# First layer: projections, attention and output projection rebuilt, with attention units taken by key group and long and short tiles in turn

## The chip, the cores and the metric

One core of one Trainium2 chip runs the whole program in one launch. The metric is the device time of that core in microseconds; the value for a kernel is the median of its runs.

## The reference, cut to what matters

The network has a first block of two layers and then a second block with routed experts. The change lies in layer 0 of the first block, up to the entry of its feed-forward part. There are 256 tokens (`x`) and 256 context rows (`ctx`), each 1024 wide, so four tiles of 128 rows.

```python
hx = rms_norm(x, norm1_g[layer]) * (1.0 + sc1) + sh1        # the same for ctx with its own sc, sh
q, k, v = split(h @ w_in)                                   # 1024 -> 16*64 | 4*64 | 4*64
q, k = rms_norm(q, q_gain), rms_norm(k, k_gain)             # per head of 64
qx, kx = apply_axial_rope(...)                              # tokens only
# tokens: 4 heads of each key group against 256 token keys (|i-j| <= 128) and 256 context keys, with a sink
# context: against the 256 context keys, with a sink
x = x + g1 * (o @ w_out);  ctx = ctx + cg1 * (oc @ w_out)
hx2 = rms_norm(x, norm2_g[layer]) * (1.0 + sc2) + sh2       # entry of conv_glu
```

`sh`, `sc` and `g` come from `silu(c) @ ada_w + ada_b`: per layer 12 column blocks of 512, so 24 weight blocks of 2 MB for both layers.

## The kernel before, in words

Weights stream through a ring of three 2 MB slots in SBUF. One queue, SyncE's, issues all loads in a written order; a load waits until the slot's previous weights have been used, and everything behind it in the queue waits too. PSUM has eight banks. `plan` code gives every group of results a number; a group uses bank number modulo 8, and TensorE's `bank(key)` waits until the reader of the group eight before has read it. `do` in the vector and scalar programs waits for each instruction's own end before the next.

Stages of layer 0, in TensorE's order:

1. Four `ada` blocks (`ada`, `ada2`): the modulation of layer 0's first norm. VectorE then squares, sums and scales the four tiles (`rms`), TensorE turns them (`turn`), ScalarE scales and shifts the turned halves (`norm_turn`, 32 instructions).
2. Projection: block 0 of `w_in` as fp32 matmuls (`stay`), blocks 1 and 2 as four half blocks of 256 columns, each product taken as three products of a high and a low part (`qw_high`, `hw_low`, `qx_high`, `qx_low`).
3. Per tile, VectorE norms the 20 heads of q and k, multiplies by the gains and applies the rotation in 12 small instructions (L1903 to L1928); TensorE turns them (L1017).
4. Attention: 16 units in the order of tiles, four key groups each. The eight of the token tiles are long (512 keys), the eight of the context tiles short (256 keys). `attention` is software pipelined: in step i TensorE does the scores of unit i, then the turning of unit i-1's exponentials and the product with v. After each unit one further `ada` block is done (`ADA_BETWEEN`). The sum of exponentials divides the result at the end (L1802).
5. The result is turned (`o0`), and the output projection (`project`) runs as fp32 matmuls of 128x512; then gate, residual sum (`residual`), norm, turn, modulation and split into high and low parts, one after another, and the feed-forward part begins at L841 with `hT_high`, `w_split`.

## Time and profile before

| | us |
|---|---|
| median of 3 runs | 2844.99 (2839.59 to 2847.72) |
| the profiled execution's own time | 2848.02 |
| its span | 2846.2 |
| TensorE busy | 2477.9 (87%) |
| VectorE busy | 974.3 (34%) |
| ScalarE busy | 775.1 (27%) |
| first matmul of the feed-forward part of layer 0 | at 495.12 |

The span is the time from the first to the last instruction of the profiled execution. "Idle before" stands in brackets behind a row of the timeline with what ended it. A busy TensorE is not TensorE at its full clock: the column PEclk tells the granted clock, 1.00 for 2.4 GHz throughout and 0.50 for 1.2 GHz.

### The profile page before, as it was taken

The page shows a single profiled execution, that of the slowest core. Times are in us where ns is not written, and L with a number is a line of the kernel's source. Part 1 is how long each engine was busy: PE and PEld are TensorE (multiplying, and loading weights), DVE is VectorE, ACT ScalarE, POOL GpSimd, SP SyncE. Part 2 cuts the span into 40 slices and gives each one's busy share as a digit, 9 for nine tenths or more (in the row PEclk, how much of TensorE's full clock was granted, in tenths as well). Part 3 has the DMA queues.
Part 4 walks back from the last instruction along what each step waited for, and adds up shares of the span by engine and source line. Part 5 has one row for each costly group of instructions (what it writes and reads, how often), then busy time and mean ns, then how long its engine had stood idle before and what let it go on. Part 6 is the DMA issues. An engine that isn't in the chain of part 4 may idle for free.

```text
span 2846.2 us, 31745 instructions
## 1 busy us (share of the span) xinstructions
PE 2477.9 (87%) x12956; PEld 1613.8 (57%) x12956; DVE 974.3 (34%) x1419; ACT 775.1 (27%) x1248; POOL 4.2 (0%) x6
## 2 busy tenths in 40 slices
PE   4939886999997997757999989799999999999995
PEld 2726653778785897654988986343333333334332
DVE  1274423334414238773654343341111111111112
ACT  2223533223314245433543453111111111111110
POOL 0000000000000000000000000000000000000000
PEclk8968997999997999887999997989999999999998
DMA  8103540442222140021555430569999999999993
GB/s 305 60 30 119 206 149 30 163 147 90 89 74 89 60 148 1 1 89 60 178 181 201 168 104 1 204 267 428 428 429 429 428 421 422 429 429 417 421 429 161
DMA packets 141897, 603.55 MB, mean 212 GB/s; under 512 B 6272, under 2 KB 51584, under 8 KB 117088
## 3 DMA queue, kind: packets, MB, share of 16 engines
q1 hardware_dynamic: 141792, 602.10, 53.5%
q8 instruction: 73, 1.20, 0.2%
q14 instruction: 32, 0.26, 0.0%
HBM read 601.03 MB, written 1.05 MB: 212 GB/s over the span
## 4 chain that ended last, share of the span: by engine, by line
PE 73%; DMA 10%; DVE 8%; ACT 6%; issue 2%; SPq 1%; ACTq 0%; DVEq 0%
PE bank L841 70%; DMA arena<-in_b_up 10%; ACT hT L1362 1%; PE bank L912 1%; DVE arena L2022 1%; ACT modp L1362 1%; ACT arena L1399 1%; DMA ring<-in_ada_w 1%; ACT arena L1387 1%; DVE xn L1742 1%; PE bank L873 0%; ACT modp L1338 0%; ACT hT L1376 0%; DVE modp L2012 0%; DVE xn L2011 0%
## 5 line engine op out<-in xcount | busy, mean ns | idle before, releaser
L841 PE MATMUL bank<-arena 128*64 128x512 f32 (+5 forms) x3088 | 644.2, 488 | 77.6 <-ACT arena L1692 25.7
L841 PEld LDWEIGHTS bank<-arena 128*64 128x64 f32 (+2 forms) x3088 | 340.5, 175 | 337.2 <-issue 267.5
L841 PE MATMUL bank<-ring,arena 128*64 128x512 f32 (+1 forms) x1632 | 394.9, 608 | 23.8 <-DMA arena<-in_b_up 21.0
L841 PE MATMUL bank<-hT_high,w_split 128*128 128x512 f32 (+1 forms) x1408 | 351.1, 341 | 30.4 <-issue 30.4
L841 PEld LDWEIGHTS bank<-ring,arena 128*64 128x64 f32 (+1 forms) x1632 | 141.3, 143 | 269.6 <-issue 259.7
L841 PEld LDWEIGHTS bank<-hT_high,w_split 128*128 128x128 f32 x1408 | 245.2, 192 | 60.6 <-issue 32.6
L841 PE MATMUL bank<-hT_low,w_split 128*128 128x512 f32 (+1 forms) x704 | 238.5, 339 | 0.0
L2159 DVE TENSOR_SCALAR arena<-bank 128x512 f32<-128x512 f32 x32 | 22.1, 692 | 549.5 <-PE bank L841 549.5
L841 PE MATMUL bank<-ring,hT 128*128 128x512 f32 (+1 forms) x432 | 182.6, 584 | 17.7 <-ACTq L666 17.7
L841 PEld LDWEIGHTS bank<-ring,hT 128*128 128x128 f32 x432 | 81.4, 195 | 116.6 <-issue 97.2
L841 PEld LDWEIGHTS bank<-hT_low,w_split 128*128 128x128 f32 x704 | 135.4, 192 | 15.3 <-issue 1.5
L755 DVE TENSOR_TENSOR w_split<-ring,w_split 128x1024 fp32r<-128x1024 f32 x88 | 107.8, 1225 | 23.2 <-ACT w_split L1417 21.3
L1417 ACT ACTIVATE w_split<-ring 128x1024 fp32r<-128x1024 f32 x88 | 93.4, 1062 | 57.9 <-PE bank L841 56.0
L2163 DVE TENSOR_SCALAR arena<-bank 128x512 f32<-128x512 f32 x32 | 22.1, 692 | 222.9 <-PE bank L841 222.9
L1688 ACT ACTIVATE arena<-arena 128x512 f32<-128x512 f32 x32 | 20.1, 629 | 246.4 <-DVE arena L2159 246.4
L841 PE MATMUL bank<-down_high,hid_high 128*128 128x512 f32 x216 | 84.9, 393 | 0.0
L841 PE MATMUL bank<-down_low,hid_high 128*128 128x512 f32 x216 | 84.0, 389 | 0.0
L841 PE MATMUL bank<-down_high,hid_low 128*128 128x512 f32 x216 | 84.0, 389 | 0.0
L1695 ACT ACTIVATE arena<-bank 128x512 f32<-128x512 f32 x32 | 19.1, 597 | 232.6 <-PE bank L841 232.6
L1679 ACT ACTIVATE arena<-bank 128x512 f32<-128x512 f32 x34 | 18.4, 594 | 208.3 <-PE bank L841 208.3
L1973 DVE TENSOR_TENSOR hw_low<-ring,hw_high 128x2048 fp32r<-128x2048 f32 x18 | 41.3, 2292 | 97.1 <-ACT hw_high L1514 96.9
L841 PEld LDWEIGHTS bank<-arena,xn 128*128 128x128 f32 x544 | 64.1, 197 | 15.5 <-issue 15.5
(307 smaller groups left out, 3418.6 us busy)
## 6 DMA issues: line engine op xcount, KB each, us to landing
ring<-in_w_gate SPq DMA_DIRECT2D x64, 2048.0 KB
arena<-in_w_down SPq DMA_DIRECT2D x64, 2048.0 KB, 15.1
ring<-in_w_up SPq DMA_DIRECT2D x32, 2048.0 KB
arena<-in_w_up SPq DMA_DIRECT2D x32, 2048.0 KB
ring<-in_ada_w SPq DMA_DIRECT2D x24, 2048.0 KB, 7.9
ring<-in_ffn_w_up SPq DMA_DIRECT2D x44, 1024.0 KB, 7.7
ring<-in_w_in SPq DMA_DIRECT2D x11, 2048.0 KB, 8.0
ring<-in_ffn_w_down SPq DMA_DIRECT2D x10, 2048.0 KB, 7.7
```

The costliest lines, as they stand in the source:

```text
L755: then(eng.tensor_tensor(w[:, 1, :, g, :], raw, w[:, 0, :, g, :].bitcast(F32), ALU.subtract))
L841: return pe.matmul(o, l, r, start=start, stop=stop)
L912: m = pe.transpose(ps[:, j * P:(j + 1) * P], pr[:, r * n + j * P:r * n + (j + 1) * P], ident)
L1362: do(act.activation(o, ps[:, j * P:(j + 1) * P], ACT.Identity, bias=modT[:, l, 24 * i + k, v:v + 1], scale=coef[:, l, i, k, v:v + 1]), F i ...
L1387: do(act.activation(PT[:, r % 2, 0:u["n"]], ps[:, 0:u["n"]], ACT.Copy), F)
L1399: do(act.activation(pr, pr, ACT.Exp, bias=st[:, 4 + r:5 + r], accum_out=st[:, 12 + r:13 + r]))
L1417: do(act.activation(w_split[fc % 2][:, 0, :, g, :], raw[:, :, g, fc % 2, :], ACT.Copy), w_high)
L1742: do(dve.tensor_tensor_reduce(out=xn[:, t % 2, :], in0=xr[:, t, :], in1=xr[:, t, :], scale=1.0, scalar=0.0, op0=ALU.mult, op1=ALU.add, acc ...
L1973: do(TT(hw_low[:, slot_of[unit_no[key]], :, 256 * z:256 * z + 256], raw, hw_high[j % 2][:, :, :].bitcast(F32), ALU.subtract), hw_low_ready)
L2022: do(dve.copy_predicated(rA[:, t, :, :], m, ps), F)
L2159: dve.tensor_scalar(hm[:, :], PS[0][:, :], 7.0, None, ALU.min).then_inc(hm_ready, 1)
L2163: link(dve.tensor_scalar(um[:, :], PS[1][:, :], 7.0, -7.0, ALU.min, ALU.max))
```

## The change

- The order of loads: x and ctx go first, the first constants are cut to 998 columns, score masks and level masks follow in front of the third block of `w_in`. The norm of x and ctx is taken before the modulation arrives, into a region of its own for each tile (`xn4`).
- Modulation of the turned tiles is shared: ScalarE takes the first halves, VectorE the second; each tile is split into high and low parts as soon as it is done.
- All three blocks of `w_in` are taken as six half blocks with the three products, keys and values first (`Q_BLOCKS`). Norm and rotation of keys run beside the projection of queries; tables of gain times cosine and sine are made once (`rope`). Queries' scale 1/rms goes into the exponential's scale (`stat` columns 0 to 63).
- Attention: units by key group, in each the tiles 0, 2, 1, 3 (token, context, token, context). Keys and queries lie in 64 rows each, so a score matmul has 64 rows (upper or lower half in turn). VectorE adds the mask and takes the maximum in one instruction. Scores of a context unit stay in their two banks until ScalarE has taken the exponentials from there (reader `exp`). The exponentials are divided by their sum before they are turned; turning goes by key chunk with four heads together, and v is the stationary operand, 64 columns at a time, so the result comes out turned and is split at once (`o_high`, `o_low`).
- The two blocks of `w_out` are loaded during attention (after units 10 and 13) and hold slots 0 and 2; the last `ada` blocks then have slot 1 alone. The output projection uses the three products. Gate, norm, turn and modulation go tile by tile behind the last output block (`enter_first`).
- For `ada` blocks that hold gates (4, 5, 10, 11) the small turning group `adat` is dropped.

```diff
+        ATT0, ATT2 = [(t, g) for g in range(NKV) for t in (0, 2, 1, 3)], list(att_units2())
 
         ADA_BETWEEN = [(0, 4 + i // 2) if i % 2 == 0 else (1, (0, 1, 2, 3, 6, 7, 8, 9)[i // 2]) for i in range(16)]
         ADA_LATE = [4, 5, 10, 11]
-        plan_att(ATT0, lambda i: plan_ada(*ADA_BETWEEN[i]))
-        plan_turn("o0", ALL)
-        for b in range(2):
-            col_unit(("wo0", b), a["attn_w_out"][0], b * 512)
-            for t in ALL:
-                add(("wo0", b, t), "dve")
+        WO_AFTER = {10: 0, 13: 1}
+
+        def out_unit(b):
+            w = a["attn_w_out"][0].rearrange("(m s j d) n -> s d m j n", m=NKV, s=2, j=2)
+            stream(("wo0", b), *[(lambda s, z=z, m=m: ring_col(s, 0, 512)[64 * z:64 * z + 64, 2 * m:2 * m + 2, :],
+                                  w[z, :, m, :, b * 512:(b + 1) * 512]) for z in range(2) for m in range(NKV)])
+
+        for i in range(len(ATT0) + 1):
+            if i < len(ATT0):
+                t, g = ATT0[i]
+                for r in range(4 if t < XT else 2):
+                    add(("score", t, g, r), "dve" if t < XT else "exp")
+            if i:
+                t, g = ATT0[i - 1]
+                l, blk = ADA_BETWEEN[i - 1]
+                ada_turn[l, blk] = len(ada_turn) % 2
+                col_unit(("ada", l, blk), a["ada_w"][l], blk * 512)
+                add(("adap", l, blk), "act")
+                for c in range(NT if t < XT else NT - XT):
+                    add(("probt", t, g, c), "act")
+                add(("pv", t, g), "dve")
+                plan_ada2(l, blk)
+                if i - 1 in WO_AFTER:
+                    out_unit(WO_AFTER[i - 1])
...
-            s = [x for x in order if x < RING - 1 or not narrow][0] if key != ("hq", 0) else RING - 1
+            held = [] if key[0] != "ada" else [slot_of[unit_no["wo0", b]] for b in range(2)
+                                               if ("wo0", b) in names[:n] and names[n - 1][0] != "up"]
+            s = [x for x in order if (x < RING - 1 or not narrow) and x not in held][0]
+            s = {("hq", 0): RING - 1, ("wo0", 0): 0, ("wo0", 1): RING - 1}.get(key, s)
...
+            early = {1: (constants,), 6: (score_masks, level_masks), 7: (gate_biases,)}
             sp.dma_start(cols[:, :], a["cols"]).then_inc(cols_landed, 16)
+            tokens()
             for n, pieces in enumerate(units):
...
+            def q_half(j):
+
+                key, z = Q_HALVES[j]
+                s = unit(key)
+                hi, lo = qw_high[j % 3], hw_low[:, s, :, 256 * z:256 * z + 256]
                 parts = [(k, *p) for k in range(KC) for p in ((hi, qx_high), (hi, qx_low), (lo, qx_high))]
+                pe.wait_ge(qw_low_ready, j + 1)
                 for t in ALL:
-                    ps = bank((*key, t))
+                    if j == 0:
+                        pe.wait_ge(qx_low_ready, t + 1)
+                    g = ("kv", t) if key[1] == 2 else ("q", key[1], t)
+                    ps = bank(g)
                     for n, (k, wt, x) in enumerate(parts):
                         m = mm(ps[:, 256 * z:256 * z + 256], x[:, k, t * P:(t + 1) * P], wt[:, k, :], n == 0,
                                n == len(parts) - 1)
                     if z:
-                        close(m, (*key, t))
-                if z:
-                    release(m)
+                        close(m, g)
+                    elif t == NT - 1:
+                        m.then_inc(q_half_used, 1)
...
+            def scores(t, g):
+                tok = slice(t * P, (t + 1) * P)
+                lo = 0 if t < XT else SEQ
+                ps = [bank(("score", t, g, r)) for r in range(4 if t < XT else 2)]
+                for r in range(4):
+                    half = slice(64 * (r % 2), 64 * (r % 2) + 64)
+                    o = ps[r][:, :] if t < XT else ps[r % 2][:, 256 * (r // 2):256 * (r // 2) + 256]
+                    m = mm(o, qT[half, 2 * g + r // 2, tok], kT[half, g, lo:TOK], True, True)
+                    if t < XT:
+                        close(m, ("score", t, g, r))
+                    elif r > 1:
+                        close(m, ("score", t, g, r - 2))
+
+            def weighted(i):
+                t, g = ATT0[i]
+                chunks = NT if t < XT else NT - XT
+                pr = P0[:, i % 2, :, :]
+                await_next(p_ready)
+                for c in range(chunks + 1):
+                    if c < chunks:
+                        ps = bank(("probt", t, g, c))
+                        for r in range(4):
+                            m = pe.transpose(ps[:, r * P:(r + 1) * P], pr[:, r, c * P:(c + 1) * P], ident)
+                        close(m, ("probt", t, g, c))
+                    if c:
+                        await_next(pt_ready)
+                        if c == 1:
+                            pv = bank(("pv", t, g))
+                        at = c - 1 if t < XT else c - 1 + XT
+                        for s in range(2):
+                            m = mm(pv[64 * s:64 * s + 64, 0:256], v0[:, at, g * HD:(g + 1) * HD],
+                                   PT0[:, (c - 1) % 2, 256 * s:256 * s + 256], c == 1, c == chunks)
+                close(m, ("pv", t, g))
+
+            for i in range(len(ATT0) + 1):
+                if i < len(ATT0):
+                    scores(*ATT0[i])
+                if i:
+                    ada(*ADA_BETWEEN[i - 1])
+                    weighted(i - 1)
+                    ada2(*ADA_BETWEEN[i - 1])
+
+            pe.wait_ge(o_low_ready, len(ATT0))
+            for b in range(2):
+                s = unit(("wo0", b))
+                for t in ALL:
+                    ps = bank(("wo0", b, t))
+                    for z in range(2):
+                        j = 2 * b + z
+                        pe.wait_ge(wo_low_ready, j + 1)
+                        hi, lo = wo_high[j], hw_low[:, s, :, 256 * z:256 * z + 256]
+                        parts = [(k, *p) for k in range(KC) for p in ((hi, o_high), (hi, o_low), (lo, o_high))]
+                        for n, (k, wt, x) in enumerate(parts):
+                            m = mm(ps[:, 256 * z:256 * z + 256], x[:, k, t * P:(t + 1) * P], wt[:, k, :], n == 0,
+                                   n == len(parts) - 1)
+                    close(m, ("wo0", b, t))
+                    if b and t:
+                        turn(("f", 0), (t - 1,), lambda t: xn[:, t % 2, :], lambda t: await_next(xn_ready))
+            turn(("f", 0), (NT - 1,), lambda t: xn[:, t % 2, :], lambda t: await_next(xn_ready))
...
+            def enter_first():
+
+                for t in range(NT + 1):
+                    if t < NT:
+                        std(t, 1)
+                    if t == 0:
+                        await_next(coef_ready)
+                    if t == 2:
+                        weights_high(0, 0)
+                    if t:
+                        norm_turn(("f", 0), (t - 1,), 0, 1, split=True, stds=False)
...
+            for i in range(len(ATT0) + 1):
+                if i:
+                    t, g = ATT0[i - 1]
+                    ada(*ADA_BETWEEN[i - 1])
+                    for c in range(NT if t < XT else NT - XT):
+                        ps = take(("probt", t, g, c))
+                        do(act.activation(PT0[:, c % 2, :], ps[:, :], ACT.Copy), F)
+                        signal(pt_ready)
+                    pe_past(("pv", t, g))
+                    do(act.activation(o_high[:, 2 * g:2 * g + 2, t * P:(t + 1) * P],
+                                      PS[group["pv", t, g] % BANKS][:, 0:256].rearrange("p (j q) -> p j q", j=2),
+                                      ACT.Copy), o_high_ready)
+                    if i - 1 in (13, 14):
+                        out_high(i - 14)
+                if i == len(ATT0):
+                    continue
+                t, g = ATT0[i]
+                st = stat[:, 64 + 32 * (i % 2):96 + 32 * (i % 2)]
+                if i == 0:
...
-                            o = kT[64 * z:64 * z + 64, z::2, t * P:(t + 1) * P]
-                            do(act.activation(o, ps[64 * z:64 * z + 64, :, :], ACT.Copy), F if z else act_step)
-            signal(qT_ready)
-
-            def with_ada(i):
-                ada(*ADA_BETWEEN[i])
-
-            attention(ATT0, with_ada)
-            plain_turn("o0", ALL)
+                        pr = P0[:, i % 2, r, 0:CTX]
+                        src = PS[group["score", t, g, r % 2] % BANKS][:, 256 * (r // 2):256 * (r // 2) + 256]
+                    at = t * NH + 4 * g + r
+                    do(act.activation(pr, src, ACT.Exp, bias=st[:, 4 + r:5 + r], scale=stat[:, at:at + 1],
+                                      accum_out=st[:, 12 + r:13 + r]))
+                if t >= XT:
...
+            def enter_first():
+
+                coefs(0, 1)
+                for t in ALL:
+                    gated_add(("wo0", 0, t), 0, t, GATE[(0, 0)], tmp=region(1024, 512))
+                for t in range(NT + 1):
+                    if t < NT:
+                        gated_add(("wo0", 1, t), 1, t, GATE[(0, 0)], tmp=region(1024, 512))
+                        rms(("f", 0), (t,))
+                    if t == NT - 1:
+                        signal(gates_read)
+                    if t == 2:
+                        weights_low(0, 0)
+                    if t:
+                        split_tokens(t - 1)
+
...
+            for i in range(len(ATT0) + 1):
+                if i:
+                    t, g = ATT0[i - 1]
+                    st = stat[:, 64 + 32 * ((i - 1) % 2):96 + 32 * ((i - 1) % 2)]
+                    n = TOK if t < XT else CTX
+                    await_next(sum_ready)
+                    do(TT(st[:, 12:16], st[:, 12:16], st[:, 8:12], ALU.add))
+                    do(dve.reciprocal(st[:, 16:20], st[:, 12:16]))
+                    for r in range(4):
+                        pr = P0[:, (i - 1) % 2, r, 0:n]
+                        do(dve.tensor_scalar(pr, pr, st[:, 16 + r:17 + r], None, ALU.mult),
+                           p_ready if r == 3 else dve_step)
+                if i < len(ATT0):
+                    t, g = ATT0[i]
+                    st = stat[:, 64 + 32 * (i % 2):96 + 32 * (i % 2)]
+                    if t < XT:
+                        for r in range(4):
+                            ps = take(("score", t, g, r))
+                            do(dve.tensor_tensor_reduce(out=P0[:, i % 2, r, :], in0=ps[:, :],
+                                                        in1=C("mask0", t * 512, 512), scale=1.0, scalar=-3e38,
+                                                        op0=ALU.add, op1=ALU.max, accum_out=st[:, r:r + 1]), F)
+                    else:
+                        for z in range(2):
+                            pe_past(("score", t, g, z))
+                            ps = PS[group["score", t, g, z] % BANKS][:, :].rearrange("p (h c) -> p h c", h=2)
+                            do(dve.tensor_reduce(st[:, z:4:2], ps, AX, ALU.max))
+                    at = t * NH + 4 * g
+                    do(TT(st[:, 0:4], st[:, 0:4], stat[:, at:at + 4], ALU.mult))
+                    do(STT(out=st[:, 4:8], in0=st[:, 0:4], scalar=-1.0, in1=minus_sink[:, 4 * g:4 * g + 4],
+                           op0=ALU.mult, op1=ALU.min))
+                    do(TT(st[:, 8:12], ROW("sink", 4 * g, 4), st[:, 4:8], ALU.add), max_ready)
+                if i:
+                    t, g = ATT0[i - 1]
+                    cut = (slice(None), slice(2 * g, 2 * g + 2), slice(t * P, (t + 1) * P))
+                    ps = take(("pv", t, g))[:, 0:256].rearrange("p (j q) -> p j q", j=2)
+                    await_next(o_high_ready)
+                    do(TT(o_low[cut], ps, o_high[cut].bitcast(F32), ALU.subtract), F)
+                    signal(o_low_ready)
+                    ada2(*ADA_BETWEEN[i - 1])
+                    if i - 1 in (14, 15):
+                        out_low(i - 15)
```

## Rows read from the trace of the kernel before

**Rows 1.** Windows: us, busy time (instructions) by engine, PEclk, DMA share, GB/s.
```profile
9.20:44.00 34.80, 20.70 (x96) 8.77 (x96) 0.69 (x4) 2.39 (x4) 0.00 (x0) 1.00 1.00 383
44.00:72.00 28.00, 7.92 (x33) 6.27 (x32) 10.04 (x19) 16.66 (x37) 0.00 (x0) 0.52 0.54 202
101.00:148.00 47.00, 46.95 (x387) 46.27 (x385) 2.98 (x2) 4.79 (x9) 0.00 (x0) 1.00 0.26 90
148.00:200.00 52.00, 11.29 (x48) 9.69 (x48) 40.30 (x56) 11.33 (x21) 0.00 (x0) 0.57 0.11 41
200.00:320.00 120.00, 107.89 (x632) 72.95 (x632) 57.41 (x106) 52.27 (x112) 0.00 (x0) 0.91 0.36 123
320.00:396.00 76.00, 66.74 (x467) 44.81 (x466) 34.50 (x93) 38.51 (x113) 0.00 (x0) 1.00 0.63 222
403.00:461.00 58.00, 56.90 (x128) 24.81 (x128) 10.51 (x16) 1.32 (x2) 0.00 (x0) 0.97 0.00 1
461.00:495.00 34.00, 7.58 (x32) 5.98 (x32) 16.08 (x27) 23.14 (x47) 0.00 (x0) 0.56 0.17 62
```
**Rows 2.** Chain that ended last, in order of time: start us, us, what.
```profile
12.22 20.52 DMA ring<-in_ada_w
72.52 75.44 PE bank L841 x448
310.71 0.82 ACT arena L1399 x2
403.13 56.91 PE bank L841 x128
476.23 0.64 ACT hT_high L1366
478.86 0.64 ACT hT_high L1366
495.12 23.87 PE bank L841 x96
```
**Rows 3.** Timeline of TensorE: start us, us, engine line op out<-in xcount.
```profile
57.85 1.97 PE L873 MATMUL bank<-const,xn 128*128 128x128 f32 x8 [0.74 <-DVE xn L1747]
241.05 1.92 PE L841 MATMUL bank<-ring,cT 128*32 128x512 f32 x16
243.74 1.05 PE L841 MATMUL bank<-const,modp 128*128 128x2 f32 x8 [0.76 <-ACTq L666]
244.65 3.68 PE L841 MATMUL bank<-arena 128*128 128x512 f32 x8
248.17 1.04 PE L912 MATMUL bank<-const,arena 128*128 128x128 f32 x8
254.10 1.92 PE L841 MATMUL bank<-ring,cT 128*32 128x512 f32 x16
```
**Rows 4.** Timeline of TensorE among the experts: operands of 64 rows, then 64 columns.
```profile
2002.29 1.99 PE L841 MATMUL bank<-arena 64*128 64x512 f32 x8
2013.01 7.07 PE L841 MATMUL bank<-ring,arena 128*64 128x512 f32 x32
```
**Rows 5.** Groups by form up to 820 us: count, busy us, mean ns, idle before.
```profile
L1783 DVE TENSOR_TENSOR arena<-bank,const 128x512 f32<-128x512 f32 x32 | 22.1, 691 | 13.8 <-PE bank L841 13.7
L1742 DVE CUSTOM_DVE_ANT_0 xn<-xr 128x1024 f32<-128x1024 f32 x8 | 9.8, 1226 | 0.3
L1747 DVE TENSOR_SCALAR xn<-xr,stat 128x1024 f32<-128x1024 f32 x8 | 6.0, 753 | 0.3
L1888 DVE TENSOR_TENSOR hw_low<-ring,qw_high 128x2048 fp32r<-128x2048 f32 x3 | 6.9, 2292 | 0.1
L1399 ACT ACTIVATE arena<-arena,stat 128x256 f32<-128x256 f32 x32 | 16.2, 508 | 1.7
L1387 ACT ACTIVATE arena<-bank 128x512 f32<-128x512 f32 x32 | 19.1, 597 | 32.9 <-PE bank L912 32.0
```
**Rows 6.** One window of layer 1's recurrence, columns as in rows 1.
```profile
1150.00:1200.00 50.00, 34.62 (x255) 32.49 (x256) 37.95 (x45) 23.95 (x50) 0.00 (x0) 0.90 0.00 1
```

563 lines of the change are left out of this document (371 added, 192 removed).

## The prediction

> **What bounds the kernel now.** I read the windows first, by stage. Only the stretch before 495.12, the first matmul of the feed-forward part, is rebuilt; what follows keeps its instructions and, but for slots 0 and 1 changing roles, its loads. In that stretch TensorE is full in three stages alone: projection (46.95 us of 47), attention (107.89 of 120, then 66.74 of 76) and output projection (56.90 of 58). Between them it is nearly empty: 7.92 of 28 us at 44 to 72, 11.29 of 52 at 148 to 200, 7.58 of 34 at 461 to 495, and there its granted clock is 0.52 to 0.57, mostly the lower level of 1.2 GHz [rows 1]. Before 44 the DMA engines are full at 383 GB/s [rows 1]; the third ada block lands at 12.22 + 20.52 = 32.74 [rows 2]. The chain passes through TensorE from 72.52 for 75.44 us and from 403.13 for 56.91 us [rows 2]. So the bounds are loads, then TensorE, and in the gaps VectorE's and ScalarE's chains.
>
> **The change part by part.** All sums are made in the profiled execution's time (span 2846.2, its own time 2848.0); the median shown lies 3.0 below that.
>
> **A, until the first projection matmul, 72.5 before.** Everything that landed before the third ada block was 11.2 MB (cols, four of constants, x, ctx and masks, three ada blocks). Now 2.0 MB of masks come later, so the fourth block is behind 11.3 MB and lands at about 33 (0.1 MB more at 0.383). Its matmuls (twice 1.92 [rows 3], at the low clock), a copy of 0.6, the small turning of 1.05 [rows 3] and coefficients 0.2 take 5.7 with issue: 38.7, less what a warm start would save, 38.2. x and ctx are already normed. TensorE turns four tiles in 4 x 1.97 [rows 3] and is through at 46.1. A half tile has a rhythm of 2.62: one split copy of 0.64 and four instructions of 0.49 [rows 2]. ScalarE now has 4 x 0.49 + 2 x 0.65 = 3.3 per tile, the other half being VectorE's, so from 40.5 the tiles are ready every 3.3 us while a tile's product takes 2.9; TensorE can start at 46.1 and never waits long. A = -26.4.
>
> **B, projection, 75.4 before** [rows 2]. Six half blocks, 4 tiles, 24 matmuls each, at 46.95 / 387 = 0.12 us [rows 1]: 69.1. Turning keys and first queries, 32 x 0.12 = 3.9. The fifth half block waits for banks of the turned keys: ScalarE has a query tile (1.3), a 1.9 us split and a copy ahead, about 2.0 net. Start at the low clock after the 0.52 stretch [rows 1]: 2.0, which is 4 us at half rate; bounds none and 6. B = 77.0, +1.6. The splits on VectorE (2.29 each [rows 5]) lie beside 11.5 us of TensorE each.
>
> **C, from the last projection to the first score, 52.1 before.** Norm and rotation of keys and of the first half of queries now lie beside B. What is left: copy and square of the last context tile 1.3, its sum 0.7, root 0.4, four copies of 0.64 (0.597 [rows 5] and issue) 2.5. C = 4.9, -47.2. If the rotation of the second queries were not hidden, 3 us more.
>
> **D, attention, 203.1 before (200.05 to 403.13).** Matmuls of 64 rows, two halves in turn, take 1.99 us per 8 of 512 columns [rows 4] against 3.68 for 128 rows [rows 3]: scores of a long unit 2.0. Products with 64 stationary columns take 7.07 / 32 = 0.22 per 512 columns [rows 4], so 0.11 for 256. ada 1.85, 16 transposes 2.0 (1.04 per 8) [rows 3]. TensorE's sum is about 9 for a long and 6 for a short unit, 15 per pair; before, a long unit took 254.10 - 241.05 = 13.05 [rows 3] and a short one about 9 (76 us for some eight and a half [rows 1]). But a chain is longer than that, because division now comes ahead of turning. Let E(i) be the end of unit i's exponentials.
>
> Step from a long unit to a short one: sum, reciprocal and four scalings of 512 at 0.42 (half of 753 ns and issue [rows 5]) 2.15; turning of the first chunk 0.7; four copies 2.6; last product 0.75; o_high 0.47; four exponentials of 256 (0.508 [rows 5] and accumulator) 2.53 and a small one 0.25: 9.45. Scaling is bounded by 0.2 (nothing in the trace so short for 512) and 0.69 [rows 5]; I take the half of L1747 since both read SBUF.
>
> Step from a short unit to a long one: the scores of a short unit stay in two banks until E. In the order of groups the `adat` or first `adag` group of the long unit before is eight behind the short unit's first score, and the next long unit's first score eight behind the second score. So TensorE stands until E and then does, in order, ada2 (1.05 [rows 3], 1.8 where it is two gate products of 512), scores 2.04, ada 1.85, turning 0.7, two copies 1.3, product 0.75, o_high 0.45, then ScalarE four exponentials of 512 at 0.845 (0.82 and issue [rows 2]) 3.4 and 0.25: 11.95, with gates 12.7. VectorE's maximum-with-mask (1226 ns for 1024 [rows 5], I take 0.8; bounds 0.6 and 0.9) is behind TensorE there and costs nothing but in the first unit.
>
> First unit 8.5; eight steps of 9.45 = 75.6; four of 11.95 and three of 12.7 = 85.9; two splits of w_out ahead of exponentials 3.9; the end, with ada2(14), ada(15) and a low-part split (2.29 [rows 5]) ahead of the last scaling, 11.0. Sum 184.9. TensorE idles some 3 us per pair in one piece, and is busy 15 of 21.7; a stage busy 34.62 of 50 is granted 0.90 [rows 6], the long units 0.91 with their cold start [rows 1]. About 8 us of a pair's chain is TensorE's; at 0.96 that is 6 us over all, at 0.90 it is 14, at 1.00 none. D = 190.9, -12.2. The loads: one 2 MB block per unit of 10 us needs 2.1 / 0.383 = 5.5 us [rows 1], so the ring keeps pace; with slot 1 alone, blocks 14 and 15 are loaded 8 us after their predecessor's use, about when wanted.
>
> **E, output projection, 56.9 before** [rows 2]: 384 matmuls at 0.12 = 46.1, -10.9 with the gap ahead. The three splits' times lie beside it.
>
> **F, to the feed-forward part, 35.0 before.** ScalarE's rhythm of 2.62 per half tile stays [rows 2]. From the end of output tile 1 (11.5 before E's end) VectorE and ScalarE go in turn: VectorE's `split_tokens(t-1)` waits for `norm_turn(t-1)`, and the next tile's gate and square wait behind it. Tile 1: gate and add 2 x 0.7 and square 1.3 ([rows 5], L1783's and L1742's kinds) 2.75, root 0.35, two half tiles 5.25, low part 0.7: 9.1; tile 2 the same and 2.2 for weights_high: 11.3; tile 3: 9.1; the last modulation 5.4. Sum 34.9, less 11.5: 23.4. F = -11.6.
>
> Sum: -26.4 + 1.6 - 47.2 - 12.2 - 10.9 - 11.6 = -106.7. 2848.0 - 106.7 = 2741.3, and against the median 2738.
>
> **The rivals.**
> (1) The banks held by the exponentials cost nothing (TensorE is ahead by other work, the step short to long falls to 10 us): 7 x about 2.2 = -15, and scaling at 0.2 gives -7 more: 2716 to 2723. For it: TensorE idled only 0.76 us ahead of the small turning in a steady unit before [rows 3]. Against: the group numbers are fixed by the plan.
> (2) The clock falls in attention. TensorE's 15 us per pair are in pieces with 2 to 3.4 us between them; the stage 148 to 200, busy 11.29 of 52, was granted 0.57 [rows 1]. With half of the pairs' time at 1.2 GHz: 8 pairs x 8 us x 0.5 = +32, less the 6 in the sum: 2764; all of it: 2796. The Trainium skill ("TensorE: Matmul & The Clock Gate", its decision table) says that throughput drops mid-kernel are avoided only without idle gaps between bursts of matmuls; by that rule the clock would fall in every pair, which is this rival. So far the trace speaks against it at this duty (0.90 at 69% busy [rows 6]).
> (3) The two row halves don't run side by side in scores: 8 long units at 3.68 in place of 2.0 [rows 3, 4], +14: 2752. [rows 4] speak against it: there the same kind of matmul in alternating halves took 0.25 each.
> (4) The held slots leave the ring without lead, and each unit waits for its ada block: a landing costs some 8 us after issue; exposed at all 16 units it is 16 x 8 = +128 and the kernel is slower, 2866. It decides from 106.7 / 16 = 6.7 us per unit. Against it: slots are held only from unit 11 on, where at most 5 units can be hit (+40: 2778).
>
> **How the numbers follow.** The forecast 0.60, (1) 0.14, (2) 0.14, (3) 0.07, (4) 0.02 in full, other mishaps 0.03. Bounds of unknown costs around the forecast: scaling -7 to +9, clock -6 to +8, A and B 5 each way. Range 2708 to 2772. A measurement here tells 0.3% or 8 us from no change; the gain exceeds it in all cases but (4) and a mishap of three figures: faster 0.96, same 0.01, slower 0.03.
>
> **What would show it.** First projection matmul at 46, first score at 128, output projection from 319 to 365, first matmul of the feed-forward part at 388. In attention, TensorE should idle before ada2 or scores with ScalarE's exponential as releaser, once per pair; pairs should take about 21.8 us, and PEclk stay above 0.9. ScalarE's and VectorE's turns after output tile 1 should be about 9 us per tile. I am wrong if the pair takes under 20 or over 25 us, if the clock there is below 0.8, or if the part after 495 before does not come out equal.

## The result and the profile after

The changed kernel takes 2778.55 us (median of 4 runs, 2776.03 to 2780.76) against 2845.52 before: ratio 0.9768 [0.975, 0.9785]. It is 67 us faster; 107 were forecast, and the range ended at 2772. The profiled execution has a span of 2778.9 and a time of its own of 2780.76, against a forecast of 2741.3 in those terms, so the miss is 39.4 us. The medians in the table of experiments take in every execution; two of them fell into a slower state, one of e12_best (4170.02 us) and one of the kernel before measured with e11_four_chunks and e12_best (4362.48), while the ratios leave such executions out.

| | before | forecast | after |
|---|---|---|---|
| first projection matmul | 72.52 | 46.1 | 45.62 |
| first score | 200.05 | 128.0 | 129.28 |
| first output-projection matmul | 403.13 | 318.9 | 363.45 |
| first matmul of the feed-forward part | 495.12 | 388.4 | 435.00 |
| from there to the end of the span | 2351.1 | 2351.1 | 2343.9 |

The row of attention is where it went wrong: 234.2 us where 190.9 were forecast and 203.1 were taken before.

The windows of after answer [rows 1], with the same columns (us, busy time by engine PE, PEld, DVE, ACT, POOL, granted clock, DMA share, GB/s). The first five are the stages, the last three a pair of units within attention.

```profile
9.20:44.00 34.80, 21.16 (x128) 10.37 (x128) 14.40 (x41) 10.03 (x17) 0.00 (x0) 0.95 1.03 381
45.60:124.00 78.40, 75.32 (x610) 74.55 (x611) 42.24 (x67) 32.57 (x51) 0.00 (x0) 0.98 0.33 119
129.60:363.40 233.80, 168.81 (x880) 78.83 (x879) 89.92 (x260) 103.83 (x228) 0.00 (x0) 0.79 0.43 138
361.00:408.00 47.00, 47.00 (x370) 46.27 (x367) 20.94 (x27) 10.57 (x16) 0.00 (x0) 0.93 0.26 90
408.00:435.00 27.00, 8.32 (x61) 7.48 (x60) 14.36 (x21) 18.71 (x36) 0.00 (x0) 0.70 0.11 39
...
244.80:251.90 7.10, 4.02 (x34) 2.07 (x32) 2.87 (x8) 4.81 (x11) 0.00 (x0) 0.96 0.84 297
251.90:268.30 16.40, 12.85 (x48) 6.98 (x48) 5.56 (x18) 5.60 (x14) 0.00 (x0) 0.60 0.53 106
268.30:279.30 11.00, 8.22 (x66) 3.74 (x64) 3.97 (x16) 6.61 (x14) 0.00 (x0) 1.00 0.62 204
```

Projection and output projection are full and hardly disturbed. Attention has a granted clock of 0.79, and it does not fall evenly: within the pair it is 0.60, so mostly 1.2 GHz, for 16.4 us and 1.00 right after. TensorE's timeline of that stretch shows what it did before (start, us, what; in brackets the idle time ahead and what ended it):

```profile
246.89 1.92 PE L899 MATMUL bank<-ring,cT 128*32 128x512 f32 x16
251.96 1.97 PE L1116 MATMUL bank<-const,arena 128*128 128x128 f32 x8 [3.14 <-DVE arena L2273]
253.86 1.12 PE L899 MATMUL bank<-arena 128*64 128x256 f32 x4
254.91 1.12 PE L1116 MATMUL bank<-const,arena 128*128 128x128 f32 x4
255.96 1.12 PE L899 MATMUL bank<-arena 128*64 128x256 f32 x4
257.01 1.12 PE L1116 MATMUL bank<-const,arena 128*128 128x128 f32 x4
258.06 1.45 PE L899 MATMUL bank<-arena 128*64 128x256 f32 x8
262.88 1.84 PE L899 MATMUL bank<-const,modp 128*128 128x2 f32 x8 [3.37 <-ACTq L717]
264.65 3.78 PE L899 MATMUL bank<-arena 64*128 64x512 f32 x8
268.36 1.92 PE L899 MATMUL bank<-ring,cT 128*32 128x512 f32 x16
```

There are two gaps in a pair. The first, 3.14, ends with the division (L2273) of a long unit's exponentials; the four divisions are 2.05 us of it. Five of the eight long units have it at 3.14 or 3.15 (the others 6.30, 1.51 and 0.16). The second, 3.37 in seven pairs, ends with ScalarE's last exponential of the short unit: these are the held banks. In this pair what comes behind each gap runs at half speed. The scores at 264.65 take 3.78 us where eight such matmuls took 1.99 in [rows 4]; the same 16 `ada` matmuls at 268.36 take 1.92 as in [rows 3], the clock being back. The long chunk row of turning and product (251.96 to 259.5) shows a second thing: TensorE takes a chunk's turning and the previous chunk's product in turn, 2.1 us a chunk, and ScalarE's copy waits for it:

```profile
253.11 0.60 ACT L1698 ACTIVATE arena<-bank 128x512 f32<-128x512 f32 x1 [3.14 <-PE bank L1116]
...
256.06 0.60 ACT L1698 ACTIVATE arena<-bank 128x512 f32<-128x512 f32 x1 [1.50 <-PE bank L1116]
258.16 0.60 ACT L1698 ACTIVATE arena<-bank 128x512 f32<-128x512 f32 x1 [1.50 <-PE bank L1116]
```

I had it the other way round, with ScalarE's 0.65 as the rhythm.

### The profile page after: what moved, and what is told of

Same layout as the page of the kernel before. It is cut to its first block, busy times and chain, and to the rows that moved or that the text cites. A ratio compares the mean times of both kernels' runs of the same rounds, so it can differ in the third digit from the quotient of the medians.

```text
span 2778.9 us, 32087 instructions
## 1 busy us (share of the span) xinstructions
PE 2432.5 (88%) x13052; PEld 1589.9 (57%) x13052; DVE 973.9 (35%) x1509; ACT 785.7 (28%) x1242; POOL 4.2 (0%) x6
## 4 chain that ended last, share of the span: by engine, by line
PE 71%; DMA 11%; ACT 8%; DVE 8%; issue 2%; SPq 0%; ACTq 0%; DVEq 0%
PE bank L899 69%; DMA arena<-in_b_up 10%; ACT arena L1720 2%; DMA ring<-in_ada_w 1%; PE bank L1116 1%; DVE arena L2395 1%; ACT modp L1486 1%; DVE arena L2273 1%; ACT arena L1698 1%; PE bank L933 1%; ACT hT L1486 1%; ACT arena L1523 1%; DVE xr L2061 0%; DVE modp L2385 0%; DVE xn L2384 0%
## 5 line engine op out<-in xcount | busy, mean ns | idle before, releaser
L899 PE MATMUL bank<-arena 128*64 128x512 f32 (+6 forms) x2896 | 616.7, 523 | 81.5 <-ACT arena L1934 25.7
L899 PEld LDWEIGHTS bank<-arena 128*64 128x64 f32 (+2 forms) x2896 | 292.3, 173 | 348.4 <-issue 269.8
L899 PE MATMUL bank<-ring,arena 128*64 128x512 f32 (+1 forms) x1632 | 394.9, 608 | 23.4 <-DMA arena<-in_b_up 21.1
L899 PE MATMUL bank<-ring,hT 128*128 128x512 f32 (+1 forms) x240 | 96.3, 563 | 2.9 <-ACTq L717 2.9
L899 PEld LDWEIGHTS bank<-ring,hT 128*128 128x128 f32 x240 | 43.9, 194 | 54.1 <-issue 50.2
## 6 DMA issues: line engine op xcount, KB each, us to landing
arena<-in_w_down SPq DMA_DIRECT2D x64, 2048.0 KB, 14.9
```

Of the source, the lines that this page charges most:

```text
L899: return pe.matmul(o, l, r, start=start, stop=stop)
```

## The experiments

My theory after the result: the shortfall in attention is the granted clock, which falls because each pair has two gaps of over 3 us, and a long-to-short step that is longer than forecast even at full clock. Rivals: the held banks alone (at any clock), the order of units itself, VectorE's division, and the `adat` groups.

In the table: the median, its ratio to the kernel before as measured beside it, the stage from about the first score to the first output-projection matmul (us) and the clock granted in it, and the steps between the starts of two units' exponentials (L long, S short). Two steps of each changed kernel also hold a split of `w_out` on ScalarE, some 1.9 us, and are not in the ranges. Stage, clock and steps are those of the one profiled execution.

| | median | ratio [95%] | stage, clock | L to S | S to L |
|---|---|---|---|---|---|
| after | 2778.55 | 0.9768 [0.975, 0.9785] | 233.8, 0.79 | 12.2 to 14.6 | 13.7 to 14.5 |
| e1_by_tile | 2751.05 | 0.9666 [0.9644, 0.9687] | 204.2, 0.87 | L to L 12.4 to 13.9 | S to S 10.7 to 11.9 |
| e2_released | 2741.69 | 0.9636 [0.9614, 0.9658] | 189.3, 0.89 | 13.2 to 14.6 | 8.8 |
| e3_warm | 2755.46 | 0.9681 [0.9659, 0.9702] | 211.0, 0.93 | 12.2 to 13.7 | 11.1 to 12.0 |
| e4_before_alternating | 2853.36 | 1.0028 [1.0016, 1.0041] | 209.6, 0.94 (before: 203.1, 0.95) | | |
| e5_one_scaling | 2755.98 | 0.9683 [0.9661, 0.9705] | 211.5, 0.85 | 10.7 to 12.5 | 12.7 to 14.3 |
| e6_adat_back | 2790.98 | 0.981 [0.9783, 0.9837] | 238.7, 0.79 | 12.2 to 14.6 | 13.7 to 16.2 |
| e7_released_by_tile | 2741.02 | 0.962 [0.9588, 0.9651] | 190.1, 0.89 | L to L 12.4 to 14.6 | S to S 8.7 to 9.2 |
| e8_released_warm | 2734.58 | 0.9598 [0.9569, 0.9628] | 184.2, 0.95 | mostly 12.2 | 8.8 |
| e9_released_by_tile_warm | 2737.04 | 0.9614 [0.9598, 0.963] | 187.0, 0.90 | L to L 12.4 to 14.4 | S to S 8.7 to 10.3 |
| e10_two_by_two | 2759.28 | 0.9696 [0.9679, 0.9712] | 212.0, 0.86 | 12.2 to 13.4; L to L 12.4 to 13.3 | 10.2 to 12.0; S to S 13.2 to 13.3 |
| e11_four_chunks | 2761.69 | 0.9714 [0.9696, 0.9731] | 214.2, 0.86 | mostly 11.2 | 12.7 to 14.9 |
| e12_best | 2721.41 | 0.957 [0.9542, 0.9599] | 180.0, 0.94 | 11.2 to 12.3 | 8.8 |

### Useless work on TensorE (e3_warm)

```diff
-                    ada(*ADA_BETWEEN[i - 1])
+                    full = ATT0[i - 1][0] < XT
+                    ada(*ADA_BETWEEN[i - 1], again=full)
                     weighted(i - 1)
+                    if full:
...
+                        for _ in range(3):
+                            mm(PS[group["adap", l, blk] % BANKS][:, :], ident, const[:, 0:512], True, True)
```

`full` is true behind a long unit. With `again`, `ada` issues its matmuls twice, the first time for nothing; the three others go into a bank whose results have been read, in the wait ahead of `ada2`.

> The changed kernel with useless TensorE work in its two gaps per pair of units: the ada block of each long unit is multiplied twice, and three matmuls of 128x512 go into the ada block's read bank before ada2 of each long unit. It computes the same. Clock theory: TensorE stands too often, the clock is granted only about 0.8 in attention and its pieces run at half rate; with the gaps filled the granted clock there is 0.95 or more and a pair falls from 27 to about 24.5 us: 2755 to 2765, faster by adding work. Rival (the clock is not what costs; the gap before ada2 ends with ScalarE's exponentials anyway): 1 to 3 us more per long unit, 2785 to 2800.

TensorE has 176 matmul instructions more to do, by the count of the trace (1056 against 880), and the kernel is 23.1 us faster than the change. The window of the stage, and a pair in TensorE's timeline:

```profile
130.50:341.50 211.00, 176.95 (x1056) 79.10 (x1057) 89.93 (x260) 103.92 (x228) 0.00 (x0) 0.93 0.47 153
```

```profile
203.74 1.02 PE L899 MATMUL bank<-const,modp 128*128 128x2 f32 x8 [0.60 <-ACTq L717]
204.69 1.99 PE L899 MATMUL bank<-arena 64*128 64x512 f32 x8
206.61 1.92 PE L899 MATMUL bank<-ring,cT 128*32 128x512 f32 x16
208.46 1.09 PE L1118 MATMUL bank<-const,arena 128*128 128x128 f32 x8
...
218.48 1.09 PE L1118 MATMUL bank<-const,arena 128*128 128x128 f32 x8 [1.42 <-DVE arena L2281]
```

The gaps are 0.60 and 1.42 now, the small turning 1.02 (after: 1.84) and the scores 1.99 (3.78). VectorE's and ScalarE's busy times are those of after, so nothing but the clock and the filled gaps can have given the time. The step S to L is 11.1 us and 12.0 with gates: the forecast's step (11.95 from end to end of two units' exponentials is 11.08 from start to start, as a short unit's are 0.87 us shorter than a long one's). So that step was sized rightly for the full clock, held banks included, and the rest of it was the clock. L to S is 12.2 at the shortest where the forecast's 9.45 is 10.3: 1.9 too short at full clock. e3 does not reach that in each step: the mean of seven is 12.9, at a granted 0.93 in the stage (0.95 or more was expected). The row halves do run side by side (1.99).

### The held banks (e2_released) and the division (e5_one_scaling)

```diff
-                    add(("score", t, g, r), "dve" if t < XT else "exp")
+                    add(("score", t, g, r), "dve")
...
-                            pe_past(("score", t, g, z))
-                            ps = PS[group["score", t, g, z] % BANKS][:, :].rearrange("p (h c) -> p h c", h=2)
+                            ps = take(("score", t, g, z))[:, :].rearrange("p (h c) -> p h c", h=2)
                             do(dve.tensor_reduce(st[:, z:4:2], ps, AX, ALU.max))
+                            do(dve.tensor_copy(P0[:, i % 2, z:4:2, 0:CTX], ps), F)
```

> The changed kernel, but VectorE copies a short unit's scores from its two banks into SBUF (two copies of 512, about 1.4 us more per short unit on VectorE) and ScalarE takes the exponentials from there, so the banks are free early. Held-bank theory: TensorE does ada2 and the long scores during the short exponentials and no longer stands 3.4 us; 7 steps lose 3 to 5 us each, and the clock is granted more than the 0.8 it has in attention: 2745 to 2760. Rival (VectorE's and ScalarE's chain is what counts, TensorE is only late because it is allowed to be): within 4 us of the changed kernel, 2775 to 2782.

VectorE has 11 us more to do (100.96 busy against 89.92) and the kernel is 36.9 us faster. The step S to L falls from 13.7 or more to 8.8; L to S does not move. TensorE's gap ahead of the small turning and the scores is gone, the one ahead of a long unit's turning is left:

```profile
212.82 1.09 PE L1116 MATMUL bank<-const,arena 128*128 128x128 f32 x8 [3.49 <-DVE arena L2269]
...
219.46 1.05 PE L899 MATMUL bank<-const,modp 128*128 128x2 f32 x8
220.44 1.99 PE L899 MATMUL bank<-arena 64*128 64x512 f32 x8
```

The seven steps S to L of the profiled execution are 37 us shorter together, which is the whole gain. In e3 the same seven steps take 82.3 us, here 63.1: 19 are the wait at full clock (2.3 a step, 3.3 where the block holds gates), which the forecast had as a cost of the change (rival (1), that it would not be there, took 15 off for it). The other 18 go with the clock, which is granted 0.89 in the stage instead of 0.79.

The other gap from the side of VectorE: the change with one of the four divisions of each unit (r = 3 alone), so the division is left out for three of four heads.

```diff
-                    for r in range(4):
+                    for r in range(3, 4):
                         pr = P0[:, (i - 1) % 2, r, 0:n]
```

> The changed kernel with one of the four scalings of the exponentials per unit (the other three heads are left undivided), to price the division ahead of the turning. If it lies on the path in every unit: 8 x 3 x 0.51 + 8 x 3 x 0.38 = 21 us less, 2757, and more where the shorter gap keeps the clock up. If it lies beside other work (TensorE's ada block in the steps after a short unit), only the long units count: 12 us less, 2766.

It gives 22.6 us, which is the number of the first expectation (2757) but not by its reason: the seven steps L to S are 18 us shorter (mostly 10.7), the steps S to L only 2, so the divisions of short units are not on the path. The three divisions of 512 are 1.5 us of 8 steps, so 12. The rest goes with the clock (0.79 to 0.85); the first gap is 1.6 us here. That the shorter gap raised the clock is argued from e3, not shown by this run.

### The order of the units (e1_by_tile, e7_released_by_tile, e10_two_by_two, e4_before_alternating)

```diff
-        ATT0, ATT2 = [(t, g) for g in range(NKV) for t in (0, 2, 1, 3)], list(att_units2())
+        ATT0, ATT2 = [(t, g) for t in ALL for g in range(NKV)], list(att_units2())
```

> The changed kernel with the attention's units in the order of before: all eight long units, then all eight short ones. Theory 1 (the order is neutral; each kind of unit has its own chain): the same time as the changed kernel, 2775 to 2782, since a short unit still holds its two banks and every unit still has one scaling, one chunk chain and one set of exponentials. Theory 2 (alternation itself costs, since after a short unit the long scores can only begin when its exponentials are done): long units no longer follow held banks, 7 steps save some 3 us each, about 2758.

> Banks released (scores of short units copied out) and units in the order of tiles, both at once. Theory 1 (alternation costs only through the held banks: between a short unit and a long one TensorE must wait for the exponentials and then do ada2, 8 score instructions and ada): with the banks released the order is neutral, the same as with the banks released alone, 2742 within 4 us. Theory 2 (alternation has a price of its own, 27 us as in the first order run): 2715.

With the banks held, long units first and short units last is 27.5 us faster than alternating. A long unit's scores then never wait for held banks, which stand only in front of other short units' scores, 1.1 us of work at full clock. And the gaps that are left are shorter, 2.29 ahead of a long unit's turning and 2.39 ahead of a short unit's scores in the timeline, where after has 3.14 and 3.37:

```profile
170.48 1.09 PE L1116 MATMUL bank<-const,arena 128*128 128x128 f32 x8 [2.29 <-DVE arena L2273]
...
280.31 1.26 PE L899 MATMUL bank<-arena 64*128 64x256 f32 x8 [2.39 <-ACTq L717]
```

With the banks released the two orders are equal: 2741.02 and 2741.69. Their intervals overlap, so what the order costs by itself is less than this comparison can tell, some 10 us; together with the held banks it costs 27.5 us. How much of that is the wait and how much the clock (0.79 against 0.87) no run separates.

Two long and two short in turn, (0, 1, 2, 3) for each group, banks held:

> The changed kernel with banks held and the order 0, 1, 2, 3 in each key group: long, long, short, short. Steps from the runs so far by kind: long to long 13.0, long to short 13.6, short to long 13.9, short to short 11.2. With 4 x (LL + LS + SS) and 3 x SL: 151 + 42 = 193, against 8 LS and 7 SL = 206 in the change: 13 us less, 2765. If only the whole order counts (all short units at the end, so that the clock stays up before): no gain, 2778.

2759.28 lies between the orders, nearer to the order of tiles than I expected. The steps are not the ones that I had added up: short to short takes 13.2 (10.7 to 11.9 in e1) and short to long 10.2 to 12.0 (13.7 or more in after), so a kind of step has no price of its own, and the sum came near by luck.

The kernel before with its units' order alone changed as in the change (the loops of `att_units0` run `for g` outside, `for t in (0, 2, 1, 3)` inside):

> The kernel before with nothing changed but the order of its attention units: by key group, tiles 0, 2, 1, 3, so long and short in turn. There scores are copied out of the banks at once and TensorE is the bound of each unit (13.05 and about 9 us). If the order is neutral in itself: the same time as before, within 4 us. If alternation costs by unlike neighbours (VectorE's long mask and maximum beside a short unit of TensorE): some 0.5 to 1 us per step, 2853 to 2860.

It is 0.28% slower [0.16, 0.41], some 8 us of 2844, at the low end of what unlike neighbours were expected to cost (2853 to 2860): in that kernel the order alone brings nothing and costs a little. In the profiled executions the stage takes 209.6 us against 203.1. What makes the difference stays open.

### The small turnings (e6_adat_back)

```diff
-            if blk not in G_BLOCKS:
-                add(("adat", l, blk), "dve")
+            add(("adat", l, blk), "dve")
```

with the same condition taken off in the two programs that use the group.

> The changed kernel with the small turning group put back for the ada blocks 4, 5, 10 and 11 of both layers. In the feed-forward part of layer 0 four such groups come back on TensorE, which is the bound there, and the stretch from its first matmul on becomes 6 to 7 us longer, as it was before. In attention four more groups of 1 us come back, of which most lie in TensorE's path: 2785 to 2792. If the 7 us after the rebuilt layer had another cause (ring slots, clock), the later part stays as short as in the changed kernel and only attention grows: 2779 to 2783.

12.4 us slower. The chain of waits of after, and of this kernel, from the first matmul of the feed-forward part:

```profile
435.00 23.98 PE bank L899 x96
461.94 22.94 PE bank L899 x98
...
539.62 269.38 PE bank L899 x1128
```

```profile
439.22 24.00 PE bank L898 x96
466.17 25.48 PE bank L898 x106
...
548.17 271.91 PE bank L898 x1136
```

With eight small matmuls more a block (x106 against x98) each of the blocks is up to 2.5 us longer: 548.17 - 439.22 = 108.95 against 104.62, and the next piece 271.91 against 269.38, together 6.9. From the first matmul of the feed-forward part to the end of the span this kernel takes 2350.6 us, before took 2351.1, after 2343.9. That is the 7.2 by which the part behind 435 came out shorter, as the four blocks with gates are also taken there and I had priced the dropped groups in attention alone. The rest of the 12.4 lies ahead of that part: 439.22 against 435.00 in the profiled executions, 4.2.

### Several together (e8_released_warm, e9_released_by_tile_warm, e11_four_chunks, e12_best)

e8 is e2 with the `ada` product of each long unit issued twice (16 useless matmul instructions), e9 the same in the order of tiles.

> Banks released, order as in the change, and the ada block of each long unit multiplied twice (1.9 us of useless TensorE work in its one remaining gap of 3.5 us per pair). It computes the same. Clock theory: the granted clock in attention rises from 0.89 to 0.97 or more and the step from a long unit to a short one falls from 13.2 to 13.8 to 12.2 everywhere, 8 x 1.3 = 10 us less than 2742: 2732. If the clock were of no weight any more once the banks are free: 2742 to 2745.

> Banks released, order of tiles, ada blocks of long units multiplied twice. If both causes, bank and clock, are all that there is, the order doesn't matter and this is as fast as released and warm in the change's order, 2730 to 2735. If consecutive long units keep the clock up by themselves, the double work brings nothing over the run without it.

Their ratios, 0.9598 [0.9569, 0.9628] and 0.9614 [0.9598, 0.963], overlap with each other and with e7's, 0.962 [0.9588, 0.9651]. So the 7 us that e8's filling shows against e2 are not settled, nor is an order. The clock in e8's stage did rise, from 0.89 to 0.95 (0.97 or more was expected), and L to S is 12.2 in five of seven steps. e9's profiled execution was its fastest, 2723.41, so its row of steps is not that of its median. One program's executions lie up to 18 us apart here (e7: 2728.16 to 2746.38), where those of after lie within 5.

e11 is the change alone with the chunk row undone:

```diff
-PT0 = region(15360, 2, 512)
+PT0 = region(15360, 4, 512)
...
-                for c in range(chunks + 1):
-                    if c < chunks:
-                        ps = bank(("probt", t, g, c))
+                for c in range(chunks):
+                    ps = bank(("probt", t, g, c))
...
+                for c in range(chunks + 1):
                     if c:
```

with `% 4` for `% 2` in the buffer's index on ScalarE and TensorE.

> The change alone, with four buffers for the turned exponentials in place of two, and TensorE turning all four chunks of a long unit before the four products. Chain theory (TensorE takes a chunk's product right behind the next chunk's turning, and the copies between decide the long-to-short step): that step falls from 12.2-14.6 us by 1.2 to 2, eight times 10 to 20 us, and the kernel takes 2760 to 2768. Rival (the exponentials and copies of ScalarE, or the granted clock alone, set that step): the same 2778 within 4.

16.9 us faster, as the chain theory had it; the rival (ScalarE or the clock alone sets the step) is out. TensorE turns the four chunks in one piece and the products follow in one:

```profile
223.00 1.97 PE L1115 MATMUL bank<-const,arena 128*128 128x128 f32 x16 [3.14 <-DVE arena L2273]
224.90 2.29 PE L899 MATMUL bank<-arena 128*64 128x256 f32 x16
230.56 1.02 PE L899 MATMUL bank<-const,modp 128*128 128x2 f32 x8 [3.38 <-ACTq L717]
231.51 3.46 PE L899 MATMUL bank<-arena 64*128 64x512 f32 x8
```

Both gaps stand as before (3.14, 3.38), but the piece between them is 4.2 us and not 7.5. L to S is 11.2 in five of seven steps, where after has 12.2 in two and 13.5 in the mean. Of the 12 us by which the seven are shorter, 7 are the shorter row (12.2 to 11.2 at full clock) and 5 are steps that now run at full clock; 5 more come from the S to L steps, which the edit does not touch. So here too more than half goes with the clock (0.79 to 0.86), and with both gaps as long as before.

e12 has all of it: e11's and e2's edits, e8's filling, and the second half of `w_out` loaded a unit later (`WO_AFTER = {10: 0, 14: 1}`).

> The change with everything that paid so far: short units' scores copied out by VectorE so that their banks come free early, four buffers for the turned exponentials with all turned first, the ada product of each long unit issued twice (the first copy is useless work that keeps TensorE busy), and wo's loads after attention steps 10 and 14. If the gains add: 2720 to 2728, against 2734.6 for released banks with the doubled ada alone. Rival (the long-to-short step is already set by ScalarE's exponentials once the banks are free): 2734 within 4.

```profile
129.10:309.10 180.00, 145.11 (x1009) 71.95 (x1009) 101.02 (x277) 104.60 (x228) 0.00 (x0) 0.94 0.56 179
```

```profile
176.53 1.05 PE L899 MATMUL bank<-const,modp 128*128 128x2 f32 x8
177.51 1.14 PE L899 MATMUL bank<-arena 64*128 64x256 f32 x8
...
183.82 1.97 PE L1117 MATMUL bank<-const,arena 128*128 128x128 f32 x16 [1.60 <-DVE arena L2271]
185.71 2.29 PE L899 MATMUL bank<-arena 128*64 128x256 f32 x16
...
188.91 1.99 PE L899 MATMUL bank<-arena 64*128 64x512 f32 x8
...
193.66 1.09 PE L1117 MATMUL bank<-const,arena 128*128 128x128 f32 x8 [0.91 <-DVE arena L2271]
...
301.16 3.64 PE L899 MATMUL bank<-ring,cT 128*32 128x512 f32 x16 [8.01 <-DMA ring<-in_ada_w]
```

It is the fastest of all. Three of its four executions took 2715.95, 2716.18 and 2726.64 us; the middle one of these is 62 us below the change and 4 below the expected 2720 to 2728. A pair is 20.0 us (27.5 in the mean in after) with gaps of 1.60 and 0.91 in the pair shown. The three gains against after, 16.9 + 36.9 + 7.1, would make 2717.7, so they add within the spread. Its ratio is clearly below that of e2; against e8 the intervals overlap ([0.9542, 0.9599] and [0.9569, 0.9628]), so what four buffers add to e8 is not settled. The later load of `w_out` has no run of its own. TensorE's longest wait in the stage is now one for the ring, 8.01 us at the end of it (last row), where after has 3.13.

## Why the prediction was wrong

**A** came out by luck, 0.5 us early. The fourth block landed when forecast (its product starts at 33.19), but the 46.1 rested on TensorE turning four tiles in 4 x 1.97 and never waiting. It turned them in one piece of 3.69 and then stood 3.61 us for the split tokens of VectorE: two errors of some 4 us that cancel.

```profile
38.31 3.69 PE L933 MATMUL bank<-const,arena 128*128 128x128 f32 x32
45.62 0.36 PE L899 MATMUL bank<-qw_high,qx_high 128*128 128x256 f32 x1 [3.61 <-DVE qx_low L2185]
```

**B and C** came out as worked: first score 1.3 late. **E and F** together are 71.6 us where 69.5 were forecast, and partly cancel: E takes 49.7 (46.1 forecast; it begins at a granted clock of 0.79 over 9.6 us and holds two turnings that the sum had left out), F 21.8 (23.4), its chain from output tile 1 on being the 34.9 of the sum but starting earlier.

**D, attention, is the step that failed**, by 43.3 us. Its parts, in the profiled execution:

- Start: 7.3 us to the first exponentials where 4.85 were forecast, +2.5.
- The 14 steps from the exponentials of unit 0 (136.6) to those of unit 14 (331.3): 194.7 where the forecast's are 7 x 10.3 + 4 x 11.1 + 3 x 11.8 + 1.95 = 154.0. At full clock the same steps take 7 x 12.2 + 4 x 11.1 + 3 x 12.0 + 1.9 = 167.7 by e3's shortest steps. So 13.7 are sizes, all of them in the step L to S, and 27.0 the clock (18 in the steps S to L, 9 in L to S), of which the forecast's sum had 6: +34.7. e3's own fourteen steps take 172.3, so 22 of the 27 are shown by a run and the rest is worked out.
- The end: 32.1 us from there to 363.45 where 26.05 were forecast, +6.1. In it stand the one wait for the ring that there is and, in the last row, a wait of 5.31 for the last short unit's exponentials. The chunk row between them is at full clock: 1.18 us from turning to turning.

```profile
334.11 3.64 PE L899 MATMUL bank<-ring,cT 128*32 128x512 f32 x16 [3.13 <-DMA ring<-in_ada_w]
...
340.50 0.66 PE L1116 MATMUL bank<-const,arena 128*128 128x128 f32 x4
...
341.68 0.65 PE L1116 MATMUL bank<-const,arena 128*128 128x128 f32 x4
...
349.02 3.75 PE L899 MATMUL bank<-modp,const 128*128 128x512 f32 x4 [5.31 <-ACTq L717]
```

**The clock** is the largest piece and is rival (2), which had 0.14 and 2764 to 2796. I took 0.96 for attention because one window at 69% busy was granted 0.90 [rows 6]. Attention is busy 72% (168.81 of 233.8) and was granted 0.79. The busy share was the wrong measure: e11 is busy 70% (150.79 of 214.2) and granted 0.86, e9 is busy 85% (158.96 of 187.0) and granted 0.90, e12 81% (145.11 of 180) and 0.94. The clock was higher where the gaps were shorter (0.6 and 1.4 in e3, 0.9 and 1.6 in e12 against 3.1 and 3.4), but the length of the gaps is not all of it either, as e11 kept both.

I had also counted one idle piece of some 3 us per pair, where there are two. And the 6 us for the clock don't follow from their own terms: 8 us of TensorE's work in each of eight pairs are 64 us, which take 2.7 us more at a granted 0.96 and 17 more at the measured 0.79. The seven pairs lost 27; in the pair shown the low clock lies on the very pieces that the chain goes through (0.60 over 16.4 us). The 2.7 and the 17 are estimates.

The Trainium skill ("TensorE: Matmul & The Clock Gate", "Why this matters for your kernels") asks for no idle gaps beyond a certain length between bursts of matmuls; the prediction told this without the length. Both gaps of after are beyond it, and by that rule the clock falls in every pair. The pair shown agrees, at 0.60 for 16.4 us, while others kept it, so that the stage as a whole, at 0.79, is between that rule and the trace of before (0.95).

**The long-to-short step** was 1.9 us short at full clock, at each of eight steps. The forecast took four copies of 0.65 as the chunk row's rhythm; it is TensorE's turning and product, 1.18 a chunk at full clock and 2.1 at half. The divisions and the exponentials were longer too:

```profile
249.85 2.05 DVE L2273 TENSOR_SCALAR arena<-arena,stat 128x512 f32<-128x512 f32 x4
...
259.97 0.56 ACT L1720 ACTIVATE arena<-bank,stat 128x256 f32<-128x256 f32 x1
...
260.66 0.56 ACT L1720 ACTIVATE arena<-bank,stat 128x256 f32<-128x256 f32 x1
...
266.92 0.69 DVE L2281 CUSTOM_DVE_ANT_0 arena<-bank,const 128x512 f32<-128x512 f32 x1
```

The divisions are 0.51 each (0.42 taken), the exponentials of 256 have a rhythm of 0.69 (0.63). VectorE's mask with maximum is 0.69 and was taken as 0.8.

**What came back**: -7.2 behind 435 by the dropped `adat` groups, not forecast. The sum: -0.5 + 1.8 + 43.3 + 2.0 - 7.2 = 39.4.

**The rivals.** (1), that the held banks cost nothing, is out: TensorE idles ahead of `ada2` with ScalarE's exponential as releaser once per pair, as forecast, and e2 prices that wait at 19 us of full clock. (3) is out by 1.99 us for eight score matmuls. (4) is out but for one wait of 3.13; that its smaller price (+40, 2778) is the measured time is chance. All three signs of being wrong that I had named came in: a pair over 25 us (27.5), a clock under 0.8 (0.79), and a part behind the feed-forward entry that is not equal (7.2 us shorter).

What stays open: why the clock is back in some pairs of one kernel and not in others with the same gaps (L to S is 12.2 in two of seven steps of after and 13.4 to 14.6 in five), why e11's clock is higher with the same gaps, and with it the spread between executions of the released kernels.

## What to carry to other kernels

Where TensorE waits on other engines in each turn of a loop, look at the length of each single gap and at what the matmuls behind it take; a busy share taken from another stage says little, and gap length alone does not settle it. Here each cure (a bank released by a copy, fewer divisions, a buffer more so that turnings run in one piece) gave about double what it took off the chain at full clock, since the clock rose with it. An order of work that alternates long and short units brought nothing in any of these kernels, and cost 27 us where the short unit held a resource that the long one was next to need.

## What the runs showed of the hardware

- 176 useless matmul instructions in attention made the kernel 23.1 us faster; the granted clock went from 0.79 to 0.93.
- Taking three of four divisions away gave 22.6 us where their own time is 12.
- An exponential with its scale and its accumulator read has a rhythm of 0.94 us for 128x512 (0.81 and a read of 0.19 that begins before its end), where 0.845 had been taken from an exponential without the scale of each row; that the scale makes the difference is not shown by a run of its own.
- VectorE's mask and maximum in one instruction takes 0.69 us and a read of 0.08 for 128x512 out of a bank, as long as a plain operation out of a bank (0.691 [rows 5]).
